# Rotary embedding in a diffusion step's attention: partner rows by ScalarE copies in a re-ordered head layout, in place of a permutation matmul

## What is computed

```python
half = A_HEAD_DIM // 2          # 32
nf = half // 2                  # 16
xr = x.reshape(x.shape[:-1] + (2, half))
x1, x2 = xr[..., :nf], xr[..., nf:]
out = jnp.concatenate([x1 * cos - x2 * sin, x2 * cos + x1 * sin], axis=-1)
...
s = jnp.einsum('bqhmd,bkhmd->bhmqk', qi, k).astype(jnp.float32) * scale
a = pr[:, :, 0] - lam * pr[:, :, 1]
```

## Time and profile before

| | |
|---|---|
| median of 3 runs | 1765.68 us (1765.24 to 1766.6) |
| the profiled execution: its own time | 1766.51 us |
| its span, first to last instruction | 1764.7 us |
| TensorE matmul busy | 1553.0 us, 88% of the span |
| VectorE busy | 479.5 us, 27% |
| ScalarE busy | 324.5 us, 18% |
| mean rate of all DMA | 291 GB/s; 427 GB/s in most of the experts' stage |

### The profile page before, as it was taken

How to read it: one execution, slowest core, us unless ns; L and a number is a source line. 1 busy time by engine, 2 the same in 40 slices (tenths; PEclk the granted TensorE clock), 3 DMA queues, 4 the chain that set the end, 5 groups by cost and what they waited for, 6 DMA issues and landing times.

```text
span 1764.7 us, 22492 instructions
## 1 busy us (share of the span) xinstructions
PE 1553.0 (88%) x9269; PEld 925.1 (52%) x9269; DVE 479.5 (27%) x1189; ACT 324.5 (18%) x893; POOL 88.0 (5%) x116
## 2 busy tenths in 40 slices
PE   6999999999999999997999887778878777977776
PEld 4655555565545555545666454444455444544443
DVE  2346778740015555424111110000110000100003
ACT  1337565610012222011100100000000000000001
POOL 0002222200000000000000000000000000000000
PEclk9999999999999999998999999999989999999999
DMA  8234344224331435284999999999999999999995
GB/s 348 78 128 167 114 139 153 90 90 189 121 108 48 191 143 203 86 328 173 396 427 427 427 427 427 428 426 426 428 416 428 427 427 427 427 428 428 427 427 228
DMA packets 40449, 512.91 MB, mean 291 GB/s; under 512 B 4624, under 2 KB 4752, under 8 KB 10528
## 3 DMA queue, kind: packets, MB, share of 16 engines
q1 hardware_dynamic: 34272, 489.89, 66.9%
q0 software_dynamic: 5936, 21.01, 3.4%
q10 hardware_dynamic: 144, 0.59, 0.1%
HBM read 506.65 MB, written 4.82 MB: 290 GB/s over the span
## 4 chain that ended last, share of the span: by engine, by line
PE 56%; DMA 32%; DVE 6%; ACT 3%; issue 2%; SPq 0%; DVEq 0%; ACTq 0%; POOL 0%
DMA arena<-in_expert_chunks 32%; PE psum L975 17%; PE psum L651 7%; PE psum L407 6%; PE psum L418 6%; PE psum L623 5%; PE psum L815 2%; PE psum L707 2%; PE psum L430 1%; ACT arena L1265 1%; PE psum L458 1%; ACT arena L1277 1%; PE psum L699 1%; PE psum L923 1%; PE psum L605 1%
## 5 line engine op out<-in xcount | busy, mean ns | idle before, releaser
L975 PE MATMUL psum<-arena 128*64 128x256 f32 x6144 | 708.6, 386 | 137.7 <-DMA arena<-in_expert_chunks 104.3
L975 PEld LDWEIGHTS psum<-arena 128*64 128x64 f32 x6144 | 442.1, 138 | 397.6 <-DMA arena<-in_expert_chunks 148.6
L2077 DVE TENSOR_TENSOR arena<-arena,psum 128x256 f32<-128x256 f32 x64 | 26.9, 421 | 704.7 <-ACT arena L1428 704.7
L407 PE MATMUL psum<-arena 128*128 128x384 f32 x512 | 171.7, 493 | 2.8 <-ACT arena L1184 2.8
L407 PEld LDWEIGHTS psum<-arena 128*128 128x128 f32 x512 | 97.6, 193 | 70.0 <-issue 6.0
L651 PE MATMUL psum<-arena 128*128 128x384 f32 x384 | 129.3, 491 | 0.0
L418 PE MATMUL psum<-arena 128*128 128x512 f32 x288 | 128.2, 601 | 0.0
L1428 ACT ACTIVATE arena<-psum 128x256 f32<-128x256 f32 x64 | 24.5, 383 | 563.6 <-PE psum L975 563.6
L1436 ACT ACTIVATE arena<-psum 32x256 f32<-32x256 f32 x126 | 47.2, 374 | 276.3 <-PE psum L975 275.2
L651 PEld LDWEIGHTS psum<-arena 128*128 128x128 f32 x384 | 72.4, 193 | 46.9 <-issue 3.0
L1062 POOL TENSOR_TENSOR arena<-arena 128x1 f32<-128x1 f32 x45 | 25.9, 577 | 1338.2 <-DVE arena L2118 944.5
(11 more groups left out here) (273 smaller groups left out, 1132.7 us busy)
## 6 DMA issues: line engine op xcount, KB each, us to landing
arena<-in_expert_chunks SPq DMA_DIRECT2D x191, 2048.0 KB, 25.4
arena<-in_mixer_chunks SPq DMA_DIRECT2D x40, 2048.0 KB, 8.3
arena<-cs_rows POOLq DMA_DIRECT2D x24, 512.0 KB, 5.3
arena<-in_h_cm POOLq DMA_DIRECT2D x8, 256.0 KB, 3.1
out_state<-arena POOLq DMA_DIRECT2D x8, 256.0 KB, 2.6
arena<-in_x_cm SPq DMA_DIRECT2D x1, 1536.0 KB, 8.8
arena<-in_expert_chunks SPq DMA_DIRECT2D x1, 1536.0 KB, 31.7
arena<-in_x_sample POOLq DMA_DIRECT2D x1, 1024.0 KB, 5.9
```

The source lines that it names most:

```text
L407: mm = pe.matmul(b[:, 0:NTOK], w[:, k, ct * P:(ct + 1) * P], src[:, k, :], start=k == 0, stop=k == KT - 1)
L975: mm = pe.matmul(psum[HALF * q:HALF * (q + 1), bank, 0:2 * P], src[:, k0 + k, :], w_k[:, 2 * P * q:2 * P * (q + 1)], start=bool(opens and ...
L2077: dve.tensor_tensor(h_sb[:, j % 2, :], sg[:, j % 2, :], psum[:, 2 + j % 2, 0:2 * P], ALU.mult)\
```

## The change

The channels of a head are laid out in another order on the host (`HEAD_ORDER`, applied to the q and k columns of the weights and to the cached keys), so that rotary partners stand 32 partitions apart. ScalarE then copies, besides the two copies that it made, the partner rows straight out of the fill's bank: four copies of 32 partitions by 256 columns into a new tile `rope_partner`. The sign goes into the sin table. TensorE's 16 permutation matmuls, the permutation constant and the two early `rope()` calls are gone. VectorE's three operations stay, but wait for `f_free`, and read `rope_partner` where they read PSUM. The context k leaves in eight DMAs of 16 partitions in place of one of 128.

```diff
-C_ID, C_TF, C_TB, C_PM, C_ON, C_COS, C_SIN, C_IO, C_END = 0, 128, 256, 384, 512, 640, 896, 1152, 1154
+C_ID, C_TF, C_TB, C_ON, C_COS, C_SIN, C_IO, C_END = 0, 128, 256, 384, 512, 768, 1024, 1026
+HEAD_ORDER = np.arange(P).reshape(2, 2, 2, A_HD // 4).transpose(0, 2, 1, 3).reshape(P)
...
-    ck = np.asarray(inputs["cache_k"])[0, 0].transpose(2, 1, 0)
+    ck = np.asarray(inputs["cache_k"])[0, 0].transpose(2, 1, 0)[HEAD_ORDER]
...
+        if name == "w_in" and c < V0:
+            block = block.reshape(D, CW // P, P)[:, :, HEAD_ORDER].reshape(D, CW)
...
+    sign = np.where(i % A_HD < half, -1.0, 1.0)[:, None]
+    c[:, C_SIN:C_SIN + 2 * P] = sign * np.sin(ang.astype(np.float32))
...
+        rope_partner = at(67, 2, 2 * P)
...
-            def rope():
-                i = n_rope[0]
-                n_rope[0] += 1
-                pe.wait_ge(sem("f_free"), ropes[i])
-                b = x_bank()
-                x_done(pe.matmul(b[:, 0:2 * P], perm, rope_raw[:, i % 2, :], start=True, stop=True))
-
...
-            rope()
-            rope()
             AT["v"] = n_p[0]
...
-                if middle.get(i, ("", 0))[0] in ("q", "k"):
-                    rope()
...
-            store(t_out["k"], kT[:, :, 0:P], ("f_free", AT["qk_last"]))
+            for p0 in range(0, P, 16):
+                d0 = int(HEAD_ORDER[p0])
+                store(t_out["k"][d0:d0 + 16], kT[p0:p0 + 16, :, 0:P], ("f_free", AT["qk_last"]))
...
-                    last = act.activation(rope_raw[:, i % 2, :], b[:, P:NTOK], ACT.Copy)
+                    act.activation(rope_raw[:, i % 2, :], b[:, P:NTOK], ACT.Copy)
+                    for p0 in range(0, P, 32):
+                        p1 = p0 ^ 32
+                        last = act.activation(rope_partner[p0:p0 + 32, i % 2, :], b[p1:p1 + 32, P:NTOK], ACT.Copy)
...
-                b = x_take()
                 dst = qT[:, h, P:NTOK] if kind == "q" else kT[:, h, 2 * P:4 * P]
+                dve.wait_ge(sem("f_free"), AT["ropes"][i])
                 c.do(dve.tensor_tensor(dst, rope_raw[:, i % 2, :], cos_t, ALU.mult))
-                x_free(dve.tensor_tensor(rope_tmp, b[:, 0:2 * P], sin_t, ALU.mult))
+                c.do(dve.tensor_tensor(rope_tmp, rope_partner[:, i % 2, :], sin_t, ALU.mult))
                 c.settle()
-                x_settle()
...
-            dve.wait_ge(sem("stored"), 32 * S_GROUPS + 32)
+            dve.wait_ge(sem("stored"), 32 * S_GROUPS + 16 + 16 * (P // 16))
```

More of the change, by code:

```diff
@@ L110, in lay_out_weights @@
     for n, (_, name, c, k, _) in enumerate(MIXER_CHUNKS):
-        mixer[n] = by_partition(np.asarray(inputs[name])[0, k * D:(k + 1) * D, c:c + CW])
+        block = np.asarray(inputs[name])[0, k * D:(k + 1) * D, c:c + CW]
+        if name == "w_in" and c < V0:
+            block = block.reshape(D, CW // P, P)[:, :, HEAD_ORDER].reshape(D, CW)
+        mixer[n] = by_partition(block)
     gate, up, down = (np.asarray(inputs[n])[0] for n in ("w_gate", "w_up", "w_down"))
@@ L132, in shape_constants @@
     half, nf = A_HD // 2, A_HD // 4
[L133 to L137, removed]
     c[:, C_ON:C_ON + P] = 1.0
@@ L141, in shape_constants @@
     inv = np.power(np.float32(10000.0), -np.arange(nf, dtype=np.float32) / np.float32(nf)).astype(np.float32)
-    axis = (i % A_HD) // half
+    axis = (i % half) // nf
+    sign = np.where(i % A_HD < half, -1.0, 1.0)[:, None]
     ang = pos[axis] * inv[i % nf][:, None]
     c[:, C_COS:C_COS + 2 * P] = np.cos(ang.astype(np.float32))
-    c[:, C_SIN:C_SIN + 2 * P] = np.sin(ang.astype(np.float32))
+    c[:, C_SIN:C_SIN + 2 * P] = sign * np.sin(ang.astype(np.float32))
     c[:, C_IO] = i
@@ L192, in build @@
         ident, tri_f, tri_b = cst[:, C_ID:C_ID + P], cst[:, C_TF:C_TF + P], cst[:, C_TB:C_TB + P]
-        perm, ones = cst[:, C_PM:C_PM + P], cst[:, C_ON:C_ON + P]
+        ones = cst[:, C_ON:C_ON + P]
         cos_t, sin_t = cst[:, C_COS:C_COS + 2 * P], cst[:, C_SIN:C_SIN + 2 * P]
@@ L658, in fill @@
                     AT["qk_last"] = n_f[0]
-            def rope():
-                i = n_rope[0]
-                n_rope[0] += 1
-                pe.wait_ge(sem("f_free"), ropes[i])
-                b = x_bank()
-                x_done(pe.matmul(b[:, 0:2 * P], perm, rope_raw[:, i % 2, :], start=True, stop=True))
-            ropes, n_rope = [], [0]
+            ropes = AT["ropes"] = []
             x_ring_is(5, 3)
```

## The result

| | before | after |
|---|---|---|
| median of 5 runs each, us | 1766.60 (1765.24 to 1770.21) | 1775.87 (1775.52 to 1777.93) |
| profiled execution, us | 1766.51 | 1776.1 |
| its span, us | 1764.7 | 1774.3 |
| TensorE busy, us (x) | 1553.0 (9269) | 1544.4 (9237) |
| ScalarE busy, us (x) | 324.5 (893) | 349.9 (957) |

The ratio is 1.0048, with a 95% interval of 1.0036 to 1.0060: slower, as forecast, but by 9.3 us (6.4 to 10.6) where 5.2 was forecast. At 1775.87 us it lies 0.9 us above the range.

The account below looks back on a forecast made before the run. TensorE's arrival at the experts' stage, which is full on weight DMA, was taken to set the end. Terms 5.5 + 2.9 + 0.9 - 0.1 - 2.4 - 1.5 = +5.2 us on 1765.68 gave 1770.9 us; range 1764.3 to 1775.0.

Parts of the forecast that it names:

- What bounds the kernel, and how a delay gets to the end: Experts' stage is full on weight DMA; whatever moves TensorE's arrival there moves the end by as much.
- The removed permutation: K step: 0.54 us of TensorE plus the gap ahead, sixteen looking like 13 us, but paying only as far as f_free allows.
- The price of the copies: Four ScalarE copies 0.389 us apart delay f_free; TensorE goes on 1.98 us after L1317's start, against 0.43 before.
- The twelve sites in the heads: Six q fills lose 0.91 us each (5.5 us) and six k fills 0.48 each (2.9 us), TensorE waiting for f_free.
- Step 1: First k fill in the attention loop, no ada_cm behind it: next scores at 539.69 against 538.77, 0.9 us lost.
- Rival 1: Partner copies overlap, 0.28 us from start to start: sum -0.8 us, 1764.9 us, not slower; chance 0.20.
- The start: First attention scores wait only for L1330, not VectorE's second rotation: 519.30 in place of 521.74, 2.4 us gained.
- With the idle time cut to under 1 us I expect the clock to hold: First q fill at the attention's start runs at full clock, 5.16 us in place of 6.66: 1.5 us gained.
- Rival 3: TensorE's clock drops in the new gaps at twelve sites and step 1, 1.5 us each: +19.5 us, 1790; chance 0.06.
- if only step 1 does: 1772.4: Milder case of the clock drop: only the 2.0 us gap in step 1 costs 1.5 us; whole rival's chance 0.06.
- Rival 2: GpSimd is late if a 16-partition k store issue exceeds 0.94 us; at 1.5 us, 4.5 us more, 1775.4; chance 0.05.
- Rival 4: Waits are absorbed later, or copies are on the chain at fewer sites: within 0.2%, about 1767; chance 0.05.

Follow-up runs that it names:

- e3: Changed kernel with the bank's f_free counted before the partner copies, which read rope_raw in SBUF: 1756.84 us, ratio 0.9937 to the kernel before.
- e4: Changed kernel with all four partner copies reading partitions 32 to 63 and writing 0 to 31 (result not the reference's): 1769.99 us, ratio 1.0015 to before.
- e5: Changed kernel with six unused identity matmuls in TensorE's gap at the end of step 1: 1774.65 us, ratio 1.0031 to before.
- e2: Changed kernel run again with nothing altered: 1773.30 us, ratio 1.0036 to before.
- e1: Kernel before the change, run again with nothing altered: 1766.26 us, ratio 0.9996.
- e11: Second run of the changed kernel with f_free counted before the partner copies, which read SBUF: 1753.78 us, ratio 0.9913 to before.

## Why the prediction was right in direction and short in size

- **What bounds the kernel, and how a delay gets to the end: right.** TensorE's arrival at the experts moved by 9.34 us (825.22 to 834.56), the loads' run by the same, and the execution's own time by 9.6.
- **The removed permutation: right.** It pays as far as `f_free` allows; with `f_free` freed (e3) the head falls 1.58 us under that of before.
- **The price of the copies: right.** 0.389 us from start to start was taken from the earlier trace rows and 0.39 was found. The head was to be 1.39 us longer and is 1.40. The twelve sites in the heads cost 8.4 us (5.5 + 2.9 forecast). Step 1 came to 1.0 (0.9 forecast): k fill to next scores is 7.62 us against 6.60.
- **Rival 1: wrong here, and its mechanism exists.** e4 shows overlapping copies, at equal partition starts. With starts 0.27 us apart the stages of e4 add up to +0.6 us over before (-2.5 at the start, +3.1 in the attention), near the 0.29 us at which the working had the sum cross zero.
- **The start: right.** -2.4 forecast, -2.50 found.
- **The step that failed: "With the idle time cut to under 1 us I expect the clock to hold. Gained: 1.5 us."** It held at the start (the first fill went from 6.82 to 5.43 us) and was lost 16 us later, behind the 1.97 us gap that the same working had put into step 1. The gate fill there pays 1.7 us (7.02 against 5.33). The net gain of the clock was 1.4 - 1.7 = -0.3 us and not 1.5. Rival 3 had named this case ("if only step 1 does: 1772.4") and I gave the whole rival 0.06. The ground against it was a mean: 1.1 us of idle time for each block of the experts at a clock of 0.97, which is itself not free of drops. This says nothing of one gap of 2 us, while the 2.32 us gap of the earlier trace rows, with a drop right behind it, was the nearest row to the 1.98 us gap of my own sum. e5 and e4 confirm that this gap made the drop. That a gap of such a length does not always make one (2.46 us in e4's state-space branch) leaves some luck in the term: with the rows of before alone it could be priced as a risk, but not as a certainty.
- **Rival 2: wrong.** An issue of 16 partitions took 0.53 us, with room for 0.94.
- **Rival 4: wrong.** Nothing was absorbed: the heads are 1.40 us longer, all thirteen sites show their wait, and from o_attn to the experts the two kernels take 117.52 and 117.57 us.
- **The size of the result.** With the moved drop the sum is 5.2 + 1.7 = 6.9 us; e2 against e1 gives 6.8. The late weights of the profiled execution, for which the working had no term, make it 7.5. The other 1.7 us of the profiled difference lie ahead of the first o_ssd matmul, where the kernels are the same, and e1 moves by 2.7 us in that place with nothing changed. These add up to the 9.3 us measured; but the stages are known of the profiled execution alone, so that the median of five is high for the same reasons is likely and not shown. The median of before had risen too, from the 1765.68 that the forecast starts from to 1766.60. I had taken 0.6 us for the spread of the runs; the medians of the changed kernel were 1775.87 and 1773.30 (e2), 2.6 us apart, those of before up to 1.4 us apart (1766.62, 1767.98), and single runs of before up to 8. The ratio's interval (6.4 to 10.6 us) holds 6.8. The upper end of the range had no term for the late weights and too small a one for the spread; that it missed by 0.9 us, and that e2's median would have lain inside, is chance.

## What to carry to other kernels

When a copy is added behind a fill, look first at which count it delays: the same four copies cost 6.8 us ahead of the bank's release and gave a kernel faster than both (0.9937 in e3 and 0.9913 in e11, the same kernel) when the bank was released first and they read SBUF. When a change removes a stretch of idle time and makes others, take each new gap against the row of the gap that had the drop, one by one, and not against a mean, and price a drop behind it as a chance. And for effects under 0.5% compare stages between marks: those touched here repeated to 0.05 us, but for a late load of weights, where totals spread by several microseconds.

## What the runs showed of the hardware that was not expected

- ScalarE's 32x256 copies start 0.39 us apart when the partition start changes from one to the next, and 0.27 us apart when it does not (e4), at 0.36 to 0.38 us each.
- TensorE's granted clock fell to 0.50 behind gaps of 2.32 us (before) and 1.97 us (after, e2), and stayed at 1.00 behind gaps of 1.61 (e4) and 1.43 us (after's heads). It also stayed at 1.00 behind one of 2.46 us in e4's state-space branch, where the same gap had a drop behind it in e2 (2.48 us). Six useless matmuls in the gap kept it up (e5), worth 1.70 us.
- From PSUM such a copy took 376 ns, from SBUF 414 ns (e3).
- With nothing changed ahead of them, executions reach the first o_ssd matmul anywhere from 380.7 to 385.1 us, and the stretch from o_attn to the experts takes either 117.5 to 117.9 or 119.8 to 120.2 us, by when the granted clock comes back in the router's stage (0.72 against 1.00 at 809 to 813 us in e3 and e11). This is as large as most of the effects studied here.
